# A two-layer decoder trunk in fp32: the high products of each weight quarter first, the low ones last, and a new split of the start-up work

## The reference

```
h = rms_norm(x) @ w_in          # 1024 x 8192 (layer 0), 1024 x 6144 (layer 1)
layer 0: HGRN2 recurrence (stage A) and block attention (stage B) on slices of h
layer 1: conv + RG-LRU (stage C) and retention (stage D) on slices of h
x += (concat(the two) * silu(z)) @ w_out
q = rms_norm(x) @ wq;  k, v = rms_norm(mem) @ wkv
x += softmax(q k^T / sqrt(128)) v @ wo
```

## Time and profile before

| | |
|---|---|
| time, median of 3 runs | 611.58 us (611.43 to 611.94) |
| the profiled execution: time | 611.41 us |
| its span in the trace | 609.6 us |
| mean granted TensorE clock | 0.993 of full speed |
| TensorE matmul busy | 589.8 us, 97% of the span |
| weight loads / VectorE / ScalarE / GpSimd busy | 540.7 / 420.3 / 382.4 / 65.2 us |
| DMA | 97.83 MB, mean 160 GB/s |

### The profile page before, as it was taken

The page is one execution under the profiler, slowest core; times in us unless marked ns, Lnnn a source line. Parts: engine busy times, 40 slices in busy tenths (PEclk is TensorE's granted clock), DMA queues, the critical chain, the costliest instruction groups (busy, mean ns, idle before and its releaser), DMA issues.

```text
span 609.6 us, 9739 instructions
## 1 busy us (share of the span) xinstructions
PE 589.8 (97%) x3913; PEld 540.7 (89%) x3913; DVE 420.3 (69%) x625; ACT 382.4 (63%) x571; POOL 65.2 (11%) x60
## 2 busy tenths in 40 slices
PE   8699999999999999999999999999999999999985
PEld 7689989999899989889988999999899998888964
DVE  3598759725985796476664876598996963766654
ACT  6385478256546757457656665859938837566762
POOL 6703001300100100100000000304110100100000
PEclk9799999999999999999999999999999999999999
DMA  9554445736454446436442833334553454256101
GB/s 289 161 187 139 139 140 162 242 101 220 127 186 138 140 154 230 169 138 212 163 178 61 286 139 139 139 139 152 203 199 139 155 217 151 100 211 237 69 2 69
DMA packets 51836, 97.83 MB, mean 160 GB/s; under 512 B 1356, under 2 KB 7760, under 8 KB 51792
## 3 DMA queue, kind: packets, MB, share of 16 engines
q1 hardware_dynamic: 51248, 96.87, 46.9%
q10 hardware_dynamic: 160, 0.27, 0.1%
q0 software_dynamic: 384, 0.08, 0.1%
HBM read 96.16 MB, written 1.05 MB: 159 GB/s over the span
## 4 chain that ended last, share of the span: by engine, by line
PE 70%; ACT 10%; DVE 9%; DVEq 4%; issue 3%; POOL 2%; ACTq 2%; POOLq 0%
PE proj L1676 11%; PE proj L1677 11%; PE proj L1678 11%; PE proj L1695 9%; PE proj L1697 9%; PE proj L1696 9%; DVE w_lo L1023 4%; PE head L1833 3%; ACT w_hi L465 3%; PE head L1922 1%; POOL prm_rows L360 1%; ACT xT_hi L487 1%; DVE work L1296 1%; ACT junk L473 1%; ACT work L854 1%
## 5 line engine op out<-in xcount | busy, mean ns | idle before, releaser
L1023 DVE TENSOR_TENSOR w_lo<-raw_weights,w_hi 128x1024 fp32r<-128x1024 f32 x174 | 223.8, 1299 | 128.9 <-ACT w_hi L465 126.7
L465 ACT ACTIVATE w_hi<-raw_weights 128x1024 fp32r<-128x1024 f32 x176 | 184.6, 1057 | 118.0 <-PE proj L1678 54.9
L1676 PE MATMUL proj<-xT_hi,w_hi 128*128 128x256 f32 x736 | 212.7, 289 | 0.7 <-DVE xT_lo L1047 0.7
L1677 PE MATMUL proj<-xT_lo,w_hi 128*128 128x256 f32 x736 | 208.2, 283 | 0.0
L1678 PE MATMUL proj<-xT_hi,w_lo 128*128 128x256 f32 x736 | 208.1, 283 | 0.0
L1676 PEld LDWEIGHTS proj<-xT_hi,w_hi 128*128 128x128 f32 x736 | 141.0, 192 | 2.7 <-issue 2.4
L1677 PEld LDWEIGHTS proj<-xT_lo,w_hi 128*128 128x128 f32 x736 | 141.1, 192 | 1.0 <-issue 0.7
L1678 PEld LDWEIGHTS proj<-xT_hi,w_lo 128*128 128x128 f32 x736 | 141.0, 192 | 0.0
L1695 PE MATMUL proj<-w_hi,y_hi 128*128 128x512 f32 x200 | 79.5, 397 | 0.0
L1697 PE MATMUL proj<-w_lo,y_hi 128*128 128x512 f32 x200 | 77.9, 390 | 0.0
L1696 PE MATMUL proj<-w_hi,y_lo 128*128 128x512 f32 x200 | 77.9, 389 | 0.0
(11 more groups left out here) (274 smaller groups left out, 752.2 us busy)
## 6 DMA issues: line engine op xcount, KB each, us to landing
raw_weights<-in_ev_w_in_dram SPq DMA_DIRECT2D x15, 2048.0 KB, 9.7
raw_weights<-in_od_w_in_dram SPq DMA_DIRECT2D x12, 2048.0 KB, 8.0
raw_weights<-in_ev_w_out_dram SPq DMA_DIRECT2D x4, 2048.0 KB, 7.8
raw_weights<-in_xa_wkv_dram SPq DMA_DIRECT2D x4, 2048.0 KB, 7.8
raw_weights<-in_od_w_out_dram SPq DMA_DIRECT2D x4, 2048.0 KB, 7.7
raw_weights<-in_xa_wq_dram SPq DMA_DIRECT2D x2, 2048.0 KB, 9.3
raw_weights<-in_xa_wo_dram SPq DMA_DIRECT2D x2, 2048.0 KB, 8.2
raw_weights<-in_ev_w_in_dram SPq DMA_DIRECT2D x4, 512.0 KB, 7.4
```

What stands on the lines that cost most here:

```text
L465: act.activation(ring_quarter(w_hi, n, q), raw_quarter(n, q), ACT.Copy).then_inc(hi_ready, 1)
L1023: dve.tensor_tensor(ring_quarter(w_lo, n, q), raw_quarter(n, q), ring_quarter(w_hi, n, q).bitcast(F32), ALU.subtract).then_inc(lo_ready, 1)
L1676: pe.matmul(dst, wh[:, k, :], x_hi[:, k, :], start=(k == 0), stop=False)
L1677: pe.matmul(dst, wh[:, k, :], x_lo[:, k, :], start=False, stop=False)
```

## The change

In `quarter_f` and `quarter_t` all products with the high part of the weight are issued first, after a wait for `hi_ready` alone, and those with the low part after a second wait. `last_half` stays as it was. At the start: GpSimd makes the low part of quarter 0 (not of quarter 1), right after the `seen` mask; the fills go to VectorE's idle beginning; ScalarE makes two pieces of `y_hi` ahead of quarter 0's high part and the other six behind it; VectorE makes the low parts of quarters 1 and 2 after its `y_lo` pieces; TensorE does quarter 2 ahead of L1769.

```diff
@@ GpSimd
+            def first_low():
+                pool.wait_ge(hi_ready, 1)
+                pool.tensor_tensor(ring_quarter(w_lo, 0, 0), raw_quarter(0, 0), ring_quarter(w_hi, 0, 0).bitcast(F32),
+                                   ALU.subtract).then_inc(first_lo, 1)
...
-            pool.memset(seen_f[:], 1.0)
-            pool.memset(scan_mask[:], 1.0)
-            pool.memset(att[:], 0.0)
-            pool.drain()
-            pool.memset(scan_mask[:].rearrange("p (c s) -> p c s", s=HGRN_CHUNK)[:, :, 0:1], 0.0)
+            pool.wait_ge(masks_filled, 1)
             for c in (0, 2 * P):
                 pool.affine_select(out=seen_f[:, c:c + P], in_=seen_f[:, c:c + P], compare_op=ALU.is_ge, fill=0.0,
                                    base=0, pattern=[[1, P]], channel_multiplier=-1)
             pool.drain()
             pool.tensor_copy(seen[:], seen_f[:]).then_inc(masks_ready, 1)
-            pool.memset(causal[:], 0.0)
+            first_low()
...
-            second_low()
             first_rows()
@@ ScalarE
-            ahead(-1, 1)
-            act.drain()
-            raw_high(range(0, 4))
+            act.drain()
+            raw_high(range(0, 2))
+            ahead(-1, 1)
+            raw_high(range(2, 8))
             ahead(-1, 2)
-            raw_high(range(4, 8))
             ahead(-1, 3)
@@ VectorE
+            dve.memset(seen_f[:], 1.0)
+            dve.memset(causal[:], 0.0)
+            dve.memset(scan_mask[:], 1.0)
+            dve.memset(att[:], 0.0)
             dve.drain()
+            dve.memset(scan_mask[:].rearrange("p (c s) -> p c s", s=HGRN_CHUNK)[:, :, 0:1], 0.0)
+            dve.drain().then_inc(masks_filled, 1)
...
-            ahead(-1, 1)
             dve.wait_ge(prm_ready, 1)
             raw_low(range(KC))
-            dve.wait_ge(second_lo, 1)
-            dve.wait_ge(hi_ready, 3)
-            dve.tensor_tensor(ring_quarter(w_lo, 0, 2), raw_quarter(0, 2), ring_quarter(w_hi, 0, 2).bitcast(F32),
+            dve.wait_ge(first_lo, 1)
+            dve.wait_ge(hi_ready, 2)
+            dve.tensor_tensor(ring_quarter(w_lo, 0, 1), raw_quarter(0, 1), ring_quarter(w_hi, 0, 1).bitcast(F32),
                               ALU.subtract).then_inc(lo_ready, 2)
+            ahead(-1, 3)
             rstd(0)
@@ VectorE: the wait for masks_ready 2 moves from before the scan of stage A to before copy_predicated
@@ TensorE, quarter_f (quarter_t alike, with both token tiles in either loop)
-                split_ready(n, q)
+                pe.wait_ge(hi_ready, 4 * n + q + 1)
...
                     pe.matmul(dst, wh[:, k, :], x_hi[:, k, :], start=(k == 0), stop=False)
                     pe.matmul(dst, wh[:, k, :], x_lo[:, k, :], start=False, stop=False)
+                low_ready(n, q)
+                for k in ks:
                     last = pe.matmul(dst, wl[:, k, :], x_hi[:, k, :], start=False, stop=(k == KC - 1))
@@ TensorE, first_slab
+                slab_f(n, [2], x=(y_hi, y_lo))
                 pe.wait_ge(diag_ready, 1)
                 pe.matmul(proj[3][:, 0:S], avg[:], memT[:, 5, :], start=True, stop=True).then_inc(rstd_psum, 1)
-                slab_f(n, [2, 3], x=(y_hi, y_lo))
+                slab_f(n, [3], x=(y_hi, y_lo))
```

More of the change, by code:

```diff
@@ L155, in hybrid_trunk @@
         out_landed = sem("out_landed")
+        masks_filled = sem("masks_filled")
         masks_ready = sem("masks_ready")
@@ L168, in hybrid_trunk @@
         raw_lo_ready = sem("raw_lo_ready")
-        second_lo = sem("second_lo")
+        first_lo = sem("first_lo")
         diag_ready = sem("diag_ready")
@@ L419, in rg_products @@
                 pool.tensor_tensor(xf, blocks(5), blocks(5), ALU.mult).then_inc(a_squared, 1)
[L421 to L425, removed]
             def first_rows():
@@ L1238, in stage_a @@
                 dve.wait_ge(lnf_ready, g + 1)
-                if g == 0:
-                    dve.wait_ge(masks_ready, 2)
                 dve.tensor_tensor_scan(wview(2), scan_mask[:], wview(0), 0.0, ALU.mult, ALU.add)
@@ L1280, in stage_a @@
                 ahead(z, 1)
+                if g == 0:
+                    dve.wait_ge(masks_ready, 2)
                 for h in range(4):
@@ L1646, in split_ready, with low_ready @@
                 pe.wait_ge(hi_ready, 4 * n + q + 1)
-                if (n, q) == (0, 1):
-                    pe.wait_ge(second_lo, 1)
+                pe.wait_ge(lo_ready, 4 * n + q + 1)
+            def low_ready(n, q):
+                if (n, q) == (0, 0):
+                    pe.wait_ge(first_lo, 1)
                 else:
@@ L1696, in quarter_t @@
                         pe.matmul(dst, x_lo[:, k0 + k, tok], wh[:, k, :], start=False, stop=False)
+                low_ready(n, q)
+                for t in range(T):
+                    dst = bank(n, t, half)[:]
+                    tok = slice(P * t, P * t + P)
+                    for k in range(2):
                         last = pe.matmul(dst, x_hi[:, k0 + k, tok], wl[:, k, :], start=False, stop=final and k == 1)
```

## The result

| | before | after |
|---|---|---|
| time, median | 611.45 us (13 runs, 610.85 to 612.01) | 613.39 us (13 runs, 613.02 to 616.10) |
| ratio after / before | | 1.0044, 95% interval 1.0031 to 1.0057 |
| the profiled execution: time, span | 611.41, 609.6 us | 613.23, 611.5 us |

The change makes the kernel 1.9 us slower by the medians, a little more than the 0.2% that can be told from no change. (The ratio goes by the means, which are 2.7 us apart.) After's times fall into two groups: eight lie at 613.0 to 613.6, five at 615.2 to 616.1, with a mean granted clock of 0.994 to 0.995 in the first and 0.988 to 0.991 in the second; their medians, 613.24 and 615.82, are 2.6 us apart. Before has one group. The profiled execution of after is one of the lower group.

The account below looks back on a forecast made before the run. TensorE, with matmuls in flight for 97% of the span, was taken as the bound, except a ScalarE/VectorE chain after L1769. Terms -1.2 - 0.7 + 2.4 = +0.5 us gave 612.1 by the median; range 609.5 to 614.4.

Parts of the forecast that it names:

- The likeliest case: Whole kernel: the summed terms as they stand, +0.5 us, giving 612.1 by the median; chance 0.47 with its bounds.
- the first rival: Start: the clock falls to half in the 3.7 us hole, costing up to 1.98 us; total +2.5, 614.1; chance 0.26.
- late low parts: Quarters where TensorE waits for a low part, at 161.90 and 429.38: high first gains 0.7 us, between 0 and 1.0.
- the sum: Whole kernel: start, late low parts and norm quarters added, +0.5 us; own range 611.2 to 613.0, chance 0.47.
- The gap at the start: TensorE's hole runs 13.4 to 17.1, 3.7 us instead of 5.7; GpSimd's drain waits for DMAs, ending at 14.14.
- With a clock that stays up: Start: condition for the 1.2 us gain, with TensorE at full pace behind the hole and L1769 ending at 25.0.
- The count of matmuls: Start: from 17.1 to L1769, 56 matmuls of 0.12 us (6.72) plus 0.49 us for two transposes.
- The rival's aside: Second idle time, 3 us ahead of L1810: the clock could fall there once more or instead.
- Norm quarters: First quarter after norms 1, 2 and 3: low products come after the late pieces, costing 0.81 us each, 2.4 in all.

Follow-up runs that it names:

- both gaps are kept busy: The kernel after plus 14 and 10 unused matmuls in TensorE's first gap and the gap ahead of L1823: 611.82 us, one group.
- the one with the low part early: The kernel after with GpSimd's first low part right behind its DMA issues, ahead of the mask work and the drain: 609.44 us.
- the order alone: The kernel before with only TensorE's order changed (high products first, low last, in every quarter), start as before: 612.28 us, ratio 1.0011.
- start alone: The kernel after with the new start kept and the interleaved order outside the first slab: 612.52 us, ratio 1.0017.

## Why the prediction was right and wrong

The range held the time (613.39 in 609.5 to 614.4). The likeliest case, 612.1, did not happen; what did is the first rival, the clock that falls in the shorter gap. That the time lies 0.7 under the rival's 614.1 is partly luck: half clock cost 0.5 less than the rival had allowed, and two further errors, of -0.5 (late low parts) and +0.39 (an idle time that I had not seen), nearly cancel. The narrower range of the sum, 611.2 to 613.0, was not worked out from its terms: their bounds give -1.2 - 1.0 + 0 = -2.2 to -1.2 - 0 + 2.9 = +1.7, so 609.4 to 613.3.

- **The gap at the start: right.** Drain's end, low part, the start at 17.1 and the fills at no cost came within 0.1 us, and the fourteen landings show that the drain waits for the DMAs.
- **"With a clock that stays up": the step that failed.** It gave 1.2 us at the start; measured, -0.18. The count of matmuls was right: the forecast had L1769's work start at 24.3, and it starts at 24.58 where both gaps are kept busy. Half clock cost 1.48 us; the rival had allowed up to 1.98. From one fall 3.2 us into a gap I had judged that 3.7 us would more often than not leave the clock up.
- **The rival's aside was right too**: the second idle time "could do the same once more". Five runs of thirteen are 2.6 us longer, of which the longer first fall and the second one explain 2.3 in the profile that has both. The diagonal's matmul behind quarter 2 makes neither gap, but it puts 2.9 us on the chain, and so sets the second one.
- **Norm quarters: right.** 0.84, 0.85 and 0.83 against 0.81 each; all 2.5 us on the path.
- **Late low parts: right in kind, mis-sized.** 1.20 against 0.7, above the upper bound of 1.0: the bound came from the two listed waits and left out the smaller ones around them. In before TensorE loses 0.72 us at 429, of which 0.48 is the listed wait, 0.22 near 435 and 0.17 near 528. The one near 161.90 is given back at 168.18, as forecast (the new kernel is 0.17 behind at 131 us and 0.10 at 168).
- **Missing: 0.39 us** from an idle time of VectorE's that six more instructions at its start moved onto the path: instruction 320 is a product with no idle time ahead of it in before, and the shuffle in after. The fills cost nothing where they stand, and something 200 us later.

By terms the forecast was -1.2 - 0.7 + 2.4 = +0.5, and the trace has +0.18 at the start, +0.39 for VectorE, -1.20 and +2.52, with -0.05 of small changes between: +1.84. The Trainium skill (TensorE: Matmul & The Clock Gate, Why this matters for your kernels) advises against idle gaps between bursts of matmuls; here the trace agrees, with 3.8 us of idling and 1.48 us of price, and its side of the rival deserved more than the 0.26 I gave.

## What to carry to other kernels

Products that don't need a late operand are the filler between waits for another late operand: put them all last only where the other operand is there. A gap of TensorE is priced with the slow matmuls behind it, and a new gap by whether the clock may fall in it, even where the same wait seems hidden. Work that another engine waits for goes ahead of a drain that has DMAs before it, and a matmul that a long chain hangs on goes ahead of those that nothing waits for.

## What the runs showed that I had not expected

- The clock's fall isn't set by a gap's length alone. A gap of 2.6 us kept full clock in after's profile and lost it in the one with the low part early; in the order alone it fell at 21.5, inside a gap of 1.6 us that follows one of 1.3. The first gap itself varies, from 3.5 to 4.5 us in the profiles with the new start and nothing to fill it, partly because quarter 0 starts anywhere from 10.3 to 11.8 in the fourteen profiles (the prediction had taken 11.44 as fixed). At half it stayed 3.4 us (after, start alone, each second fall) or 6.8 us (before, and four of the experiments at the start). Why one execution has the one and the next the other stays open, as does why both falls come together in the upper group.
- VectorE's idle times of 0.37 to 0.56 us at fixed places of its instruction stream. The Trainium skill (Runtime: NRT & Kernel Launch, Instruction fetch mechanics) has each engine's instruction memory refilled in blocks by a DMA queue of its own, mostly hidden. The trace agrees with the blocks: the idle times stand 128 or a multiple of 128 instructions apart, a packet of the instruction queue stands next to one of them and moves with it, and at the other places of this count (192, 576 and 704 in after) no idle time shows. The packet comes after the idle time has ended (217.13), so what VectorE waits for there is only argued.
- Eight no-operations on VectorE did not move its stream, and the trace has no record of them; nine real instructions moved it by nine.
